# Two transformer blocks on one core: half of the k tiles of gate and up as seven products of sums, in the whole of each group

## The reference, cut to what matters

```python
hn2 = rmsnorm(x, norm2_w[l])
gu = hn2 @ w_gate_up[l]                      # 2048 x 11264
x = x + (jax.nn.silu(gu[..., :FFN_HIDDEN]) * gu[..., FFN_HIDDEN:]) @ w_down[l]   # FFN_HIDDEN = 5632
```

## Time and profile before

| | us |
|---|---|
| median of 3 runs | 2576.79 (2575.72 to 2576.93) |
| the profiled execution, its own time | 2576.22 |
| its span, first to last instruction | 2574.4 |
| around the span | 1.8 |
| PE busy | 2561.0 (99%) |
| DVE, ACT, POOL busy | 1603.7, 1473.3, 824.6 |
| granted TensorE clock | 1.000 of full speed |
| gate and up, groups 1 to 10 | about 794 to 1217, and 1908 to 2332 |

### The profile page before, as it was taken

How to read it: one execution, slowest core, us unless ns; L and a number is a source line. 1 busy time by engine, 2 the same in 40 slices (tenths; PEclk the granted TensorE clock), 3 DMA queues, 4 the chain that set the end, 5 groups by cost and what they waited for, 6 DMA issues and landing times.

```text
span 2574.4 us, 30659 instructions
## 1 busy us (share of the span) xinstructions
PE 2561.0 (99%) x11740; PEld 2122.9 (82%) x11740; DVE 1603.7 (62%) x1799; ACT 1473.3 (57%) x1811; POOL 824.6 (32%) x368
## 2 busy tenths in 40 slices
PE   9999999999999999999999999999999999999999
PEld 7888888888887888888888888888878888888887
DVE  6798955434347878787533467456477878786222
ACT  7776645445455656566544575565565656566333
POOL 2687753344441000000444455333320000003443
PEclk9999999999999999999999999999999999999999
DMA  8766654466666475656566644554557565655554
GB/s 302 222 209 204 178 192 161 162 223 210 204 203 246 168 250 174 243 184 217 190 215 205 223 168 157 172 196 142 185 194 247 174 243 183 234 194 194 202 203 147
DMA packets 174705, 516.13 MB, mean 200 GB/s; under 512 B 108027, under 2 KB 111068, under 8 KB 117216
## 3 DMA queue, kind: packets, MB, share of 16 engines
q1 hardware_dynamic: 174128, 513.64, 59.9%
q10 hardware_dynamic: 432, 0.52, 0.1%
HBM read 487.38 MB, written 2.10 MB: 190 GB/s over the span
## 4 chain that ended last, share of the span: by engine, by line
PE 94%; DVE 2%; issue 1%; ACT 1%; POOL 1%; DMA 0%; SPq 0%; ACTq 0%; DVEq 0%; POOLq 0%
PE PB L858 18%; PE PB L862 18%; PE PB L859 18%; PE PB L925 8%; PE PB L926 8%; PE PB L929 8%; PE PB L909 2%; PE PB L906 2%; PE PB L904 2%; ACT WH L1460 1%; PE PB L1168 1%; PE PB L1010 0%; DVE WL L2251 0%; PE PB L1040 0%; POOL WL L3321 0%
## 5 line engine op out<-in xcount | busy, mean ns | idle before, releaser
L3321 POOL TENSOR_TENSOR WL<-RAW,WH 128x1024 fp32r<-128x1024 f32 x280 | 703.1, 2512 | 1730.0 <-ACT WH L1460 1729.1
L1460 ACT ACTIVATE WH<-RAW 128x1024 fp32r<-128x1024 f32 x738 | 776.2, 1057 | 797.6 <-PE PB L862 634.3
L2251 DVE TENSOR_TENSOR WL<-RAW,WH 128x1024 fp32r<-128x1024 f32 x456 | 613.6, 1348 | 753.6 <-ACT WH L1460 752.3
L858 PE MATMUL PB<-WH,HNH 128*128 128x512 f32 x1152 | 458.6, 398 | 2.6 <-ACT TM L2036 2.4
L862 PE MATMUL PB<-WL,HNH 128*128 128x512 f32 x1152 | 449.4, 390 | 1.5 <-POOL WL L3321 1.5
L859 PE MATMUL PB<-WH,HNL 128*128 128x512 f32 x1152 | 448.6, 389 | 0.0
L858 PE MATMUL PB<-WH,HDH 128*128 128x512 f32 x704 | 273.9, 389 | 0.0
L859 PE MATMUL PB<-WH,HDL 128*128 128x512 f32 x704 | 273.9, 389 | 0.0
L862 PE MATMUL PB<-WL,HDH 128*128 128x512 f32 x704 | 273.9, 389 | 0.0
L858 PEld LDWEIGHTS PB<-WH,HNH 128*128 128x128 f32 x1152 | 216.4, 188 | 50.5 <-ACT TM L2036 3.2
L862 PEld LDWEIGHTS PB<-WL,HNH 128*128 128x128 f32 x1152 | 216.2, 188 | 49.0 <-POOL WL L3321 3.4
(11 more groups left out here) (450 smaller groups left out, 3887.0 us busy)
## 6 DMA issues: line engine op xcount, KB each, us to landing
RAW<-in_w_gu SPq DMA_DIRECT2D x136, 1024.0 KB, 7.2
RAW<-in_w_dn SPq DMA_DIRECT2D x88, 1024.0 KB, 4.8
RAW<-in_w_in_a SPq DMA_DIRECT2D x53, 1024.0 KB, 5.2
RAW<-in_w_in SPq DMA_DIRECT2D x45, 1024.0 KB, 4.8
RAWX<-in_w_gu SPq DMA_DIRECT2D x40, 1024.0 KB, 6.6
RAW<-in_w_out SPq DMA_DIRECT2D x32, 1024.0 KB, 4.7
RAW<-in_w_ga SPq DMA_DIRECT2D x24, 1024.0 KB, 4.8
RAW<-in_w_gb SPq DMA_DIRECT2D x24, 1024.0 KB, 4.8
```

Of the source, the lines that this page charges most:

```text
L858: e.matmul(o, hi[:, k, x], WH[:, s, c], start=k == 0, stop=False)
L1460: e.activation(wh(key), source(key), ACT.Copy).then_inc(*wt.act.mark(("wh", *key)))
L2251: e.tensor_tensor(to, raw, hi, ALU.subtract).then_inc(*wt.dve.mark(("wl", *key)))
L3321: e.tensor_tensor(to, raw, hi, ALU.subtract).then_inc(*wt.pool.mark(("wl", *key)))
```

## The change

Two parts of four are now sums, over 8 of the 16 k tiles, in all ten groups: the blocks b11, b22, t1, t2, b21, t3 go first, each in two pieces (c = 0, 1), then up of d = 2, t4, gate of d = 2 and 3, and up of d = 3. A group has 22 pieces instead of 19. A group uses four banks, x, y, z, w, and the next group the other four; b11, t2, t3 and t4 all go to bank x in turn, and ScalarE copies it out (`part`) before the next adds to it. VectorE's instructions on products are six instead of ten, ScalarE's six instead of three, with `up_columns` of a group at k == 3 of the next. Loads come in another order (`gate_up_order`: up 0, gate 0, up 1, gate 1, up 2, gate 2, gate 3, up 3). There are five raw buffers, and loads stand six places ahead. Three pairs of places for split weights need room: X (2 MB) is written to DRAM in group 0 ("x away", k == 50), and read back at the start of the down product ("x back", k == 12).

```diff
-BLOCKS = ("b11", "b21", "b22", "t1", "t2", "t3", "t4")
-BANK_OF = (1, 2, 3, 5, 6, 7, 4)
-SUMMED = (1,)
-SUM_BEHIND = {0: 3, 2: 4, 3: 5, 4: 6}
+BLOCKS = ("b11", "b22", "t1", "t2", "b21", "t3", "t4")
+BANK_OF = {"b11": "x", "b22": "y", "t1": "z", "t2": "x", "b21": "w", "t3": "x", "t4": "x"}
+SUM_BEHIND = {("b11", 0): (("t1", 0),), ("b11", 1): (("t1", 1),), ("b22", 1): (("t2", 0),), ("t1", 0): (("t2", 1),), ("t1", 1): (("t3", 0),), ("t2", 0): (("t3", 1),),
+              ("b21", 0): (("t4", 0),), ("b21", 1): (("t4", 1),)}
...
+        items = [(b, c) for b in BLOCKS[:6] for c in range(2)] + [(("up", 2), c) for c in range(2)]
+        items += [("t4", c) for c in range(2)] + [((of, d), c) for of, d in (("gate", 2), ("gate", 3), ("up", 3)) for c in range(2)]
+        takes = [6 if b in BLOCKS else 12 for b, c in items]
+        starts = [-(-128 * sum(takes[:i]) // sum(takes)) for i in range(len(items))]
+        place_in_group = [("up", 0), ("gate", 0), ("up", 1), ("gate", 1), ("up", 2), ("gate", 2), ("gate", 3), ("up", 3)]
...
-        loaded = [(-1, 0)] * (NRAW + 1)
+        loaded = [(-1, 0)] * (NRAW + 2)
...
-            raw_due.setdefault(16 * (n - (5 if n in wider else 4)) + 1, []).append(n)
+            raw_due.setdefault(16 * (n - (6 if n in wider else 4)) + 1, []).append(n)
...
+        def banks_summed(j, nt):
+
+            if j % 2:
+                return {"x": PB[3], "y": mb(nt), "z": mb(nt + 1), "w": mb(nt + 2)}
+            return {"x": PB[4], "y": PB[5], "z": PB[6], "w": PB[7]}
...
+                elif p in wider and wider[p][3] < 2:
+                    stage, j, of, d = wider[p]
+                    e.wait_ge(*low_half(stage, j, {("up", 0): "t1", ("gate", 0): "t3", ("up", 1): "t2", ("gate", 1): "t4"}[of, d], 1))
+                    if of == "up":
+                        e.wait_ge(*wt.dve.done("sum", stage, j, ("t4" if d else "t2"), 1))
...
                     for k in tiles(128):
+                        if j == 0 and k == 50:
+                            for h in range(2):
+                                e.wait_ge(*m.dve.done("x", before, 3, h))
+                            e.dma_start(AWAY[:, :, :], X[:, :, :]).then_inc(landed["x away"], 16)
                         if j and k == 36:
...
+            def x_back(stage):
+                e.wait_ge(*wt.pe.done("nt", NT[{1: "gu1", 3: "gu2"}[stage]] + 43))
+                e.dma_start(X[:, :, :], AWAY[:, :, :]).then_inc(landed["x back"], 16)
...
+                    if c == 0 and block in ("t2", "t3", "t4"):
+                        e.wait_ge(*m.act.done("part", stage, j, {"t2": "b11", "t3": "t2", "t4": "t3"}[block]))
...
-                    if k == 54:
-                        sums_rounded()
...
+                for k in tiles(64):
+                    if k == 6:
+                        sums_rounded()
+                def part(j, block, to, *before):
+
+                    banks = banks_summed(j, NT[gu] + 4)
+                    e.wait_ge(*wt.pe.done("unit", stage, j, block, 1))
+                    if before:
+                        e.wait_ge(*before)
+                    e.activation(to, banks[BANK_OF[block]][:, :], ACT.Copy).then_inc(*m.act.mark(("part", stage, j, block)))
+
                 for j in range(1, 11):
                     for k in tiles(128):
+                        if k == 10:
+                            part(j, "b11", CP[:, 0, :], *(m.dve.done("taken", stage, j - 1, "w") if j > 1 else ()))
                         if k == 16:
                             hidden_split(j - 1)
+                        if k == 28:
+                            part(j, "t1", flat(ST[:, :, :]), *(m.dve.done("taken", stage, j - 1, "y") if j > 1 else ()))
+                        if k == 36:
+                            part(j, "t2", CP[:, 1, :], *(m.dve.done("taken", stage, j - 1, "z") if j > 1 else ()))
+                        if k == 53:
+                            part(j, "t3", CP[:, 1, :], *m.dve.done("u4", stage, j))
                         if k in (74, 82):
                             hidden_joined(j - 1, (k - 74) // 8)
+                        if k == 113:
+                            e.wait_ge(*wt.pe.done("product", stage, j, "x"))
+                            e.wait_ge(*m.act.done("planes", "z", stage, j - 1, 1))
+                            e.activation(SIG[:, 1, :], banks_summed(j, NT[gu] + 4)["x"][:, :], ACT.Silu, scale=RTOK[:, 1:2]).then_inc(
+                                *m.act.mark(("silu", stage, j, 1)))
...
                 for j in range(1, 11):
                     for k in tiles(128):
+                        if j > 1 and k == 3:
+                            up_columns(j - 1)
+                        if k == 42:
+                            less_u2(j)
+                        if k == 109:
+                            first_columns(j)
...
-        for d in range(4):
-            yield 8 * j + d
-            yield 8 * j + 4 + d
+        for i in (4, 0, 5, 1, 6, 2, 3, 7):
+            yield 8 * j + i
```

More of the change, by code:

```diff
@@ L869, in summed_group @@
                 nt = NT[gu] + 4
-                banks = {2: mb(nt), 3: mb(nt + 1), 4: mb(nt + 2), 1: PB[3], 5: PB[4], 6: PB[5], 7: PB[6], 8: PB[7]}
+                banks = banks_summed(j, nt)
                 def bank_free(q):
[L873 to L876, removed]
+                    if j > 2:
+                        e.wait_ge(*(m.act.done("silu", stage, j - 2, 1) if q == "x" else m.dve.done("taken", stage, j - 2, q)))
+                    elif j == 1 and q != "x":
+                        main_free(nt + "yzw".index(q))
                     else:
@@ L921, in plain @@
+                def plain(of, d, c):
+                    u, = key = key_of(stage, j, (of, d), c)
+                    for h in range(2):
+                        q, x = {"gate": "wx", "up": "yz"}[of][h], slice(h * 128, (h + 1) * 128)
+                        if (of, d, c, h) == ("up", 2, 0, 1):
+                            e.wait_ge(*m.act.done("part", stage, j, "t1"))
                         if h == 0:
@@ L934, in plain @@
                             t.then_inc(*wt.pe.mark(*steps))
-                for d in range(4):
-                    (seven if d in SUMMED else plain)(d)
+                for n in w.tiles(128):
+                    if n in starts:
+                        what, c = items[starts.index(n)]
+                        if what in BLOCKS:
+                            of_sums(what, c)
+                        else:
+                            plain(*what, c)
             def turn(name, src, g, wait):
@@ L2054, in ffn @@
+                        if k == 116:
+                            e.wait_ge(*m.dve.done("taken", stage, j, "w"))
+                            e.activation(SIG[:, 0, :], SIG[:, 0, :], ACT.Silu, scale=RTOK[:, 0:1]).then_inc(
+                                *m.act.mark(("silu", stage, j, 0)))
                         if j == 10 and k in (100, 108):
@@ new lines, in less_u2, with up_columns @@
+                def less_u2(j):
+                    e.wait_ge(*m.act.done("part", stage, j, "t1"))
+                    e.wait_ge(*m.act.done("part", stage, j, "t2"))
+                    u4 = flat(ST[:, :, :])
+                    e.tensor_tensor(u4, u4, CP[:, 1, :], ALU.subtract).then_inc(*m.dve.mark(("u4", stage, j)))
+                def up_columns(j):
+                    banks, u4 = banks_summed(j, NT[gu] + 4), flat(ST[:, :, :])
+                    e.wait_ge(*wt.pe.done("product", stage, j, "y"))
+                    e.wait_ge(*m.dve.done("u4", stage, j))
+                    e.tensor_tensor(u4, banks["y"][:, :], u4, ALU.add).then_inc(
+                        *m.dve.mark(("y", stage, j), *([("free", NT[gu] + 43)] if j == 9 else [])))
+                    e.wait_ge(*wt.pe.done("product", stage, j, "z"))
+                    e.wait_ge(*m.act.done("part", stage, j, "t3"))
+                    e.tensor_tensor(CP[:, 1, :], banks["z"][:, :], CP[:, 1, :], ALU.subtract).then_inc(
+                        *m.dve.mark(("z sum", stage, j), *([("free", NT[gu] + 41)] if j == 9 else [])))
```

308 lines of the change are left out of this document (127 added, 181 removed).

## The result

| | before | after |
|---|---|---|
| median of 4 runs, us | 2576.86 (2575.72 to 2577.36) | 2623.89 (2618.92 to 2626.21) |
| ratio, 95% interval | | 1.0181 (1.0163 to 1.0198) |
| the profiled execution, its own time and span, us | 2576.22, 2574.4 | 2626.11, 2624.3 |

The account below looks back on a forecast made before the run. A loop over SyncE, ScalarE and VectorE was to bound each group: 0.55 + 11.0 + 1.1 + 30.6 = 43.25 us. That gave +11.4 in both stages, +14 in all on 2576.8: 2591 us, range 2560 to 2625.

Parts of the forecast that it names:

- this ring: Loop over SyncE, ScalarE and VectorE from t4's second low to the next group's: 43.25 us per group, more than 40.8.
- X to the turn's issue: X is the end of t4's second low; from there to SyncE issuing z's two transposes (the turn): 0.55 us.
- from this low to X: VectorE from b11's low to the end of t4's second low, with no idle time: 30.6 us.
- the paragraph on where PE feels it: PE's t3 waits until ScalarE's queue frees bank x; PE stands idle about 2.4 us per group.
- the third of the ring: SyncE's queue from issuing z's transposes until gate 0's weights land: transposes hold the queue, then the load; 11.0 us.
- the one-load row: Profile reading with one load right ahead of z's transposes: 5.35 us holding the queue, 10.65 from issue to gate 0's landing.
- the sum: Whole kernel: +11.4 us in both stages, silu's wait -2.4, row sums +4, read-back +1; so +14 on 2576.8.
- The rival of two loads' backlog: Two earlier loads count fully before gate 0 lands, 12.6 us or more: 44.85 per group, 2620 us; chance 0.15.
- The quick turn: z's transposes to gate 0's landing under about 9.9 us; z's path through ScalarE binds: 2563, hidden 2550; chance 0.16.
- VectorE starting each instruction only at the end of the one before: VectorE from b11's low to t4's: 2.1 us more, 2629 us; within the two-load case's chance of 0.15.
- The clock: PE's clock falls to 1.2 GHz for 5 us after each stall: +50, 2641 us; chance 0.02.
- Wrong would be ... a clock below 1: Sign in the profile after that would show the forecast wrong: PE's granted clock under 1, the 2.4 GHz level.

Follow-up runs that it names:

- run 1: The changed kernel with the two transposes of z moved from k == 36 to k == 0, ahead of the group's loads in SyncE's queue: 2562.38 us, ratio 0.9947.
- run 3: The changed kernel with the second lows of gate 3 and up 3 given to GpSimd in each group: 2621.87 us, ratio 1.0178.
- run 5: The changed kernel with the lows of t3 and up 2 computed on 512 of 1024 columns of each piece: 2592.81 us, ratio 1.0066.
- run 7: The changed kernel with nearly all gate and up loads bringing 1024 of 2048 columns, order untouched: 2565.57 us, ratio 0.9958.
- run 11: The kernel of run 10 with the loads of gate 0 and up 0 exchanged: 2698.07 us, ratio 1.0472.
- run 10: The kernel of run 1 with `up_columns` at k == 0 instead of 3 on VectorE: 2551.41 us, ratio 0.9903.
- run 8: The changed kernel with the loads of gate 0 and up 0 exchanged, gate 0 first: 2629.42 us, ratio 1.0207.
- run 9: The kernel of run 1 with ScalarE's split of z moved from k == 16 to k == 37: 2590.20 us, ratio 1.0055.
- run 4: The changed kernel with both lows of up 2 given to GpSimd in each group: 2696.40 us, ratio 1.0466.

## Why the prediction was right or wrong

**Right.** It said slower, because of this ring, and runs 1, 3, 5 and 7 bear that out: to shorten the turn, the landing or VectorE's work within the ring shortens the pitch, and VectorE's work outside it does nothing. Of the ring's terms, X to the turn's issue was 0.54 us (0.55 predicted), ScalarE's b11 to VectorE's low 1.09 (1.1), and from this low to X 30.62 or 30.63 in all nine rounds of the first stage (30.6). The latter holds the 24 instructions at 1.135 us. The estimate of 1.224 us by the formula of the Trainium skill ("VectorE: DVE Perf Modes", section on the TRN2 errata) fits the duration shown, 1.22 or 1.23, and not the distance of starts. PE waited before t3 for ScalarE's copy, as the paragraph on where PE feels it says, and its waits in the groups were 2.6 us per group (2.4). Silu's wait is gone.

**The step that failed** is the third of the ring, "From the turn's issue to gate 0's landing ... I take 11.0". From the turn's issue to ScalarE's start on b11 it was 11.86 in the group shown, and between 11.85 and 14.5 in the others of the first stage; worked out from the pitch it is 45.11 - 0.54 - 1.09 - 30.62 = 12.9 us on average. The turn alone held the queue for 6.06 to 8.51 us, 7.0 on average, where the one-load row has 5.35; from its end to b11 it was another 5.8 us, where that row has 5.3. The mechanism was right and the term was 1.9 us too small: 9 x (45.11 - 43.25) = 16.7 us in the first stage and 9 x (44.94 - 43.25) = 15.2 in the second, 31.9 of the 2626.1 - 2590.2 = 35.9 us that the sum missed of the profiled execution.

**The last 4 us** lie ahead of the ring: the first X of a stage comes 3.2 us later than the sum has it. I count from a low of VectorE in group 0 that both kernels have, at 748.60 before and at 747.56 after. Group 1 of the kernel before begins 46.2 us behind it (its first down product, 1217.52, less 422.7). With the terms of the sum, X comes at 46.2 + 16.5 + 2 - 1.2 (silu's wait) = 63.5 us; it came at 66.7 (814.24). In the second stage it was 73.4 for 70.2. VectorE's work on the row sums grew there by some 5.6 us (from 6.2 to 11.8), and I had allowed 2 us for it; that this is the cause is likely, not shown. Against these 6.4 us stand 1 us for reading X back, which cost nothing (the two kernels are 25.2 us apart at the start of the first down product and 25.15 in group 0 of the second stage), and the 1 us by which the kernel after is ahead at 747.56.

**Why it was too small.** I had two rows, 12.6 with two loads right ahead and 10.65 with one, and chose near the one-load row because the two other loads were issued 4 to 5 us before. For the turn they count for the most part: its 7.0 us stand nearer to the 7.49 of two loads than to the 5.35 of one, and in run 11, with one load right ahead and none 4 us before, it takes 5.46. That the bytes matter is shown by run 7, where the same span is 8.14 us, though it also has half the bytes in gate 0's own load. The rival of two loads' backlog, at 12.6 and 2620 us, was the case that came; it had a chance of 0.15. The range held the measurement by 1 us at its upper end, which is owed to that rival and not to the sum. What makes the turn take 6.1 us in one group and 8.5 in another, with loads at the same distances ahead, stays open.

**The other rivals.** The quick turn did not come by itself, but its two figures can be read in runs made for it: 41.5 us per group over z and ScalarE (run 1: 41.42) and 40.8 with that hidden (run 10), 2563 and 2550 us against 2562.4 and 2551.4. VectorE starting each instruction only at the end of the one before is ruled out by the 30.63. **The clock** did fall: to 0.80 in the window of 936 to 953, and within it to 0.50 from 944 to 948, which is the 1.2 GHz level; PE had just waited 0.52 and 1.92 us. I had given this 0.02 as a loss of its own. It cost little or nothing in this group, since the distance from b11's low to X stayed at 30.62 us in it too: PE has 4.3 us to spare per group, and a slower PE only waits less. "Wrong would be ... a clock below 1" was thus too strong a sign. So was "PE for VectorE's lows of b11 or t2": PE did wait for lows of t2, up to 3.12 us, and in that round too the distance was 30.62, since VectorE had no gap.

**A small miss.** The sum for after has no term for PE's wait for the z of group 0, 1.1 us in each stage. It stayed. VectorE sets the first X there, so by the same sum it costs nothing. And of the two waits of the earlier trace rows the one for silu stands in group 0 (775.36), and not around the start of group 1 as I read it; nothing in the sum hangs on that.

## What to carry to other kernels

A queue that issues DMAs in order is a chain like any engine. When loads are moved earlier or buffers are added, list for each issue in the queue what it waits for, and put an issue whose data is ready early ahead of a load that waits for the busiest engine; above all a transpose, which keeps the queue for longer the more is under way. After such a list, look which buffer each load takes, since an exchange of two loads gives later ones other buffers (runs 8 and 11), and see that the issue put ahead is not itself late (run 9). An engine that is busy for 65% of the span can be part of the bound: look for a ring by the pitch of one instruction, and price only what lies in it.

## What the runs showed of the hardware

- **An issue of two transposes of z holds SP's queue by what is under way:** 2.59 us with nothing near (run 1), 3.93 us with loads of half size (run 7), 5.46 us with one 1 MB load right ahead (run 11), 5.86 to 8.54 us with one right ahead and two some 4 us before (the change), up to 10.55 us in run 8.
- **GpSimd slows VectorE:** a float32 subtraction on 128 x 1024 of VectorE, both inputs in SBUF, takes 3.38 us instead of 1.22 while GpSimd runs its own (run 4), and 2.60 us in run 3.
- **TensorE's clock:** in the kernel after PE waits 2.6 us per group, and the granted clock was 0.80 over one stretch of 17 us (936 to 953) and 0.993 over the execution. Behind two waits of 0.52 and 1.92 us it was 0.50 from 944 to 948, and matmuls began 427 ns apart instead of 227; by 952 to 956 it was 1.00 again. The same two waits one group earlier (before 896.86 and 899.98) left it at 1.00, so such a wait does not always lower it. The mean was 1.000 before and in run 10, where such waits are missing, and 0.980 and 0.982 in the two slowest kernels.
